# A hybrid mixer with its norms, keys, values and attention laid out anew, in a residual block on one core

## What is computed

```python
proj = einsum('btd,dc->btc', rmsnorm(x), w_in)        # 2048 -> 7184 columns
# attention, blocks of 128 queries, q, k, v raw:
z = q @ k.T * scale; valid = s_idx < t_idx
log_1m = where(valid, log_sigmoid(-z), 0)
later = cumsum(log_1m, reverse=True) - log_1m
att = where(valid, exp(log_sigmoid(z) + later), 0)
o_sb = rmsnorm(att @ v, sb_out_gain)
# delta rule: q, k, v through a width-4 convolution and silu; q and k L2-normed
g = cumsum over the chunk of the log gates; decay = exp(g_i - g_j)
L = where(strict, (k * beta) @ k.T * decay, 0)
T_mat = inverse(I + L); u = T_mat @ (v * beta); w = T_mat @ (k * beta * exp(g))
# per chunk: v_new = u - w @ S; o = (q * exp(g)) @ S + qk @ v_new; S updated
o_dn = rmsnorm(o, dn_out_gain) * silu(dn_z)
h = x + rmsnorm(concat(o_sb, o_dn) @ w_out)
```

## Time and profile before

| | us |
|---|---|
| median of 3 runs | 1363.92 (1348.13 to 1617.84) |
| the profiled execution | 1355.06 |
| its span | 1353.3 |
| PE busy | 1294.6 (96%) |
| DVE busy | 940.7 (70%) |
| ACT busy | 708.2 (52%) |
| POOL busy | 228.8 (17%) |
| moved by DMA | 225.85 MB, mean 167 GB/s |

### The profile page before, as it was taken

One profiled execution on the slowest core, in us unless ns is written; L12 is line 12 of the kernel. 1 busy time (PEld: TensorE's weight loads), 2 busy tenths in 40 slices (PEclk: granted clock), 3 DMA queues, 4 the chain that ended last, 5 costly groups with the idle time before them and its releaser, 6 DMA issues.

```text
span 1353.3 us, 20838 instructions
## 1 busy us (share of the span) xinstructions
PE 1294.6 (96%) x6906; PEld 1088.4 (80%) x6906; DVE 940.7 (70%) x1703; ACT 708.2 (52%) x1288; POOL 228.8 (17%) x293
## 2 busy tenths in 40 slices
PE   5999979999999979989999999999999999999996
PEld 4676769857888757878888888888888888888885
DVE  5697696646765535566978888888788885555554
ACT  5454444424434664546566656665666555444442
POOL 5321120122201130000222322232222220000000
PEclk9899989979999988999999999999999999999999
DMA  8352543313633403553555455554555556555551
GB/s 329 124 204 108 139 175 119 131 63 123 199 116 127 167 19 125 191 183 124 191 201 197 178 194 187 186 190 182 206 176 202 179 199 221 197 202 188 187 186 62
DMA packets 32695, 225.85 MB, mean 167 GB/s; under 512 B 4352, under 2 KB 4736, under 8 KB 5888
## 3 DMA queue, kind: packets, MB, share of 16 engines
q1 hardware_dynamic: 30528, 218.12, 45.2%
q10 hardware_dynamic: 2112, 7.00, 2.1%
HBM read 222.87 MB, written 2.23 MB: 166 GB/s over the span
## 4 chain that ended last, share of the span: by engine, by line
PE 87%; DVE 8%; ACT 2%; issue 1%; DMA 1%; ACTq 1%; POOL 0%; DVEq 0%; SPq 0%; POOLq 0%
PE bank L1219 35%; PE bank L1221 17%; PE bank L1508 8%; PE bank L1510 8%; PE bank L1509 8%; DVE w_lo L752 3%; ACT w_hi L409 1%; DVE arena L777 1%; PE bank L1302 1%; PE bank L1255 1%; PE bank L1373 1%; PE bank L1313 1%; PE bank L1273 1%; DVE ssum L822 1%; DMA raw<-in_wts 1%
## 5 line engine op out<-in xcount | busy, mean ns | idle before, releaser
L1219 PE MATMUL bank<-xhl,w_hi 128*128 128x512 f32 x2304 | 826.6, 403 | 21.3 <-DVE w_lo L752 15.9
L752 DVE TENSOR_TENSOR w_lo<-raw,w_hi 128x512 fp32r<-128x512 f32 x816 | 574.9, 727 | 250.2 <-ACT w_hi L409 248.0
L409 ACT ACTIVATE w_hi<-raw 128x512 fp32r<-128x512 f32 x816 | 500.4, 628 | 392.2 <-PE bank L1221 233.8
L1221 PE MATMUL bank<-xhl,w_lo 128*128 128x256 f32 x2304 | 645.7, 280 | 0.0
L1219 PEld LDWEIGHTS bank<-xhl,w_hi 128*128 128x128 f32 x2304 | 437.3, 190 | 140.3 <-issue 20.8
L1221 PEld LDWEIGHTS bank<-xhl,w_lo 128*128 128x128 f32 x2304 | 438.8, 190 | 0.1
L1508 PE MATMUL bank<-w_hi,ffn_act 128*128 128x512 f32 x352 | 136.9, 389 | 0.0
L1510 PE MATMUL bank<-w_hi,ffn_act 128*128 128x512 f32 x352 | 136.9, 389 | 0.0
L1509 PE MATMUL bank<-w_lo,ffn_act 128*128 128x512 f32 x352 | 136.9, 389 | 0.0
L381 POOL TENSOR_TENSOR arena<-arena,token_scale 128x256 f32<-128x256 f32 x88 | 79.4, 918 | 308.8 <-DVE arena L757 186.4
L1141 DVE SCALAR_TENSOR_TENSOR arena<-arena,fcw 128x256 f32<-128x256 f32 x176 | 85.3, 485 | 23.9 <-DVE arena L1141 1.5
(11 more groups left out here) (230 smaller groups left out, 847.1 us busy)
## 6 DMA issues: line engine op xcount, KB each, us to landing
raw<-in_wts SPq DMA_DIRECT2D x204, 1024.0 KB, 4.7
xfeat<-in_x SPq DMA_DIRECT2D x4, 512.0 KB, 9.5
xfeat<-in_x_tok ACTq DMA_DIRECT2D x1, 2048.0 KB, 7.8
arena<-base_rows ACTq DMA_DIRECT2D x16, 128.0 KB, 5.0
out_y<-xfeat SPq DMA_DIRECT2D x4, 512.0 KB, 2.9
arena<-in_post_gains ACTq DMA_DIRECT2D x1, 1024.0 KB, 4.7
down_gain<-in_post_gains ACTq DMA_DIRECT2D x1, 1024.0 KB, 4.7
arena<-in_w_ba ACTq DMA_DIRECT2D x1, 320.0 KB
```

The source lines that it names most:

```text
L409: nc.scalar.activation(w_hi[:, i % RING, :], raw[:, slot, quarter * PIECE:(quarter + 1) * PIECE], ACT.Copy).then_inc(hi_ready, 1)
L752: V.tensor_tensor(w_lo[:, i % RING, :], raw[:, slot, quarter * PIECE:(quarter + 1) * PIECE], w_hi[:, i % RING, :].bitcast(f32), ALU.subtra ...
L1219: M(ps[j][:, :], w_hi[:, r % RING, w], xhl[:, k, :, :].rearrange("p a t -> p (a t)"), start=(k == 0), stop=False, skip_group_check=True)
L1221: last = M(ps[j][:, 0:T], w_lo[:, r % RING, w], xhl[:, k, 0, :], start=False, stop=(k == KT - 1), skip_group_check=True)
```

## The change

It rewrites the mixer; nothing that is computed changes, but nearly every step's layout and place does.

- **Token groups.** `FEAT_GROUPS = 10`: the first ten input groups (dn q, k, v of batch 0, the same of batch 1, sb q and k) stay feature pieces. The last four (sb v, two groups; dn z, two groups) become token pieces, in banks (0,1) and (2,3) in turn. ACT alone empties these, two 512-wide operations a group that also apply the token's norm, and silu for z (`token_evac`, L471).
- **Input.** ACT rounds x times its gain in one operation, DVE forms the rest in one; POOL has no part in it. The sum of squares of x comes from a token-major copy of x (ACT, 2 x 2048 elements with accumulation), and one 256-column matmul at slot 18 spreads it.
- **Gates.** 64 matmuls of 32 or 16 columns at slot 14 give logits with tokens on partitions; beta, gates, their sums and the norms are then columns `col[128 x 16]`. Gate differences come back through DRAM as a broadcast load.
- **Norms.** Keys are not normed: the factors go into the triangular system (`CNEG`), with squares from transposed keys (ACT, accumulating, L1361 for the transposes). Sums with 8 columns and spreads with 8 rows (L1293, L1302, L1313, L1263, L1420, L1465, L1524) are gone.
- **Batches** start at slots 44 and 112. The block loads are 2 instead of 8 a batch. Spreading the base blocks (L374) and level masks (L332) are on POOL, 512 wide. The first tap of each convolution is on ACT.
- **Attention** runs in two rounds of four heads from slots 181 and 200, between token pieces. Its output is token-major, normed there, transposed back (16 transposes); the same for z times o (`z_turn`, one batch at slot 214, one inside the first output group). The output projection reads a tile of its own, `mix_hl`.

```diff
-            def conv_tile(g, j):
...
-                    else:
-                        ins = V.tensor_scalar(conv[:, j, :], proj[:, t, :], w, None, ALU.mult)
-                    ins.then_inc(s("conv_done") if lag == 3 else s("conv_step"), 1)
+            def conv_tile(c, j):
...
+                dve.wait_ge(s("conv_first"), n_ + 1)
+                for lag in range(1, 4):
...
+            def token_evac(g):
...
+                    dst, func = (vtok, ACT.Copy) if n_ < 2 else (ztok, ACT.Silu)
+                    nc.scalar.activation(dst[:, j, 512 * (n_ % 2):512 * (n_ % 2) + 512], ps[token_banks(g)[j]][:, :], func,
+                                         scale=stat[:, 3, j:j + 1]).then_inc(s("tok_evac"), 1)
...
+            follow(PLACE["ba"])
+            pe.wait_ge(s("wba_lo"), 1)
...
+                for k in range(KT):
+                    M(ps[5][:, 64 * j:64 * j + 32], xhl[:, k, 0, js], wba_hl[:, k, :, :].rearrange("p a n -> p (a n)"),
+                      start=(k == 0), stop=False, skip_group_check=True)
+                    last = M(ps[5][:, 64 * j:64 * j + 16], xhl[:, k, 1, js], wba_hl[:, k, 0, :],
+                             start=False, stop=(k == KT - 1), skip_group_check=True)
...
+                for g in range(2):
+                    follow(PLACE["kt", b, g])
...
+                    turn(lambda r: chunk(1, 4 * g + r), ps[4 + g], "kt_mm")
+                    follow(PLACE["kk", b, g])
...
+                        last = M(ps[6 + g][:, r * P:(r + 1) * P], k_, k_, start=True, stop=True)
...
-            follow(SB_PLACE)
-            pe.wait_ge(s("sbq"), HEADS)
...
-            for h in range(EARLY):
-                sb_z(h)
-            follow(16 * IN_GROUPS)
+            for r in range(BATCHES):
+                heads = range(BH * r, BH * r + BH)
+                for h in heads:
+                    sb_z(h)
+                pe.wait_ge(s("tri_ready"), 2)
+                for h in heads:
+                    sb_c(h)
+                for h in heads:
+                    sb_av(h)
...
-            for i in range(HEADS // 2):
-                pe.wait_ge(s("son_rstd"), 1)
-                for a in range(2):
-                    last = M(ps[4 + i][:, a * T:(a + 1) * T], sel[:, 2 * i + a, :], nrow, start=True, stop=True)
-                last.then_inc(s("son_bc"), 1)
```

More of the change, by code:

```diff
@@ L50, in down_bank @@
     return (4 + 2 * c + j) % 8
[L53 to L56, removed]
-    for _i in range(BASE):
[L58 to L69, removed]
-    for _i in range(2 * LEVELS):
[L71 to L74, removed]
+PLACE = {"ba": 14, "stat": 18, "gcum": 24, "grow": 26, "gload": 28}
@@ L493, in step @@
                 act_e.wait_ge(s("act_step"), n[0])
+            follow(PLACE["stat"] + 2)
             act_e.wait_ge(s("ba_sb"), 1)
-            nc.scalar.activation(small[:, 0, :], small[:, 0, :], ACT.Exp, scale=-1.0).then_inc(s("eb"), 1)
-            step(nc.scalar.activation(small[:, 1, :], small[:, 1, :], ACT.Identity, bias=gate[:, 1:2]))
-            step(nc.scalar.activation(small[:, 2, :], small[:, 1, :], ACT.Abs))
-            step(nc.scalar.activation(small[:, 3, :], small[:, 2, :], ACT.Exp, scale=-1.0))
@@ L530, in _ @@
+                for g in range(2):
+                    follow(PLACE["turn", b, g] + 1)
                     act_e.wait_ge(s("turned"), 2 * b + g + 1)
@@ L559, in sb_exp @@
+                for u in range(UNITS):
+                    ins = nc.scalar.activation(squares[:, u, :], otok[b][:, u, :], ACT.Square, accum_out=c_(OO, 8 * b + u))
+                ins.then_inc(s("o_sq"), 1)
+                follow(PLACE["rs", b] + 1)
+                act_e.wait_ge(s("o_inv"), b + 1)
+                nc.scalar.activation(col[:, RS, block_n(b)], col[:, RS, block_n(b)], ACT.Sqrt).then_inc(s("o_root"), 1)
             def sb_exp(h):
@@ L1272, in _ @@
-            for k in range(KT):
-                last = M(ps[5][0:40, 0:T], wba[:, k, :], full[:, k, :], start=(k == 0), stop=(k == KT - 1))
-            last.then_inc(s("ba_done"), 1)
-            follow(40)
-            pe.wait_ge(s("bg_row"), 1)
-            pe.wait_ge(s("ke_row"), 1)
-            for n_, (r, j) in enumerate(((1, 0), (1, 1), (0, 0), (0, 1), (2, 1), (3, 0))):
-                last = nc.tensor.transpose(ps[6][:, 8 * n_:8 * n_ + 8], rows[:, r, j * P:(j + 1) * P], ident[0:8, 0:8])
@@ new lines, in sb_ot, with z_turn @@
+            def sb_ot(h):
+                follow(PLACE["ot", h])
+                pe.wait_ge(s("so_tok"), h + 1)
+                for j in range(NJ):
+                    js = slice(j * P, (j + 1) * P)
+                    last = nc.tensor.transpose(ZB[h % BH][:, T + j * P:T + (j + 1) * P], SO_TOK[h % BH][:, js], ident[:, :])
+                last.then_inc(s("ot_mm"), 1)
+            def z_turn(b, g):
+                pe.wait_ge(s("z_mix"), 2 * b + g + 1)
+                turn(lambda r: otok[b][:, 4 * g + r, :], ps[2 * b + g], "zturn_mm")
```

1496 lines of the change are left out of this document (771 added, 725 removed).

## The result

The changed kernel takes 1294.55 us (median of 4, 1293.84 to 1295.3), the kernel before 1356.03 (median of 4). The ratio is 0.956, with a 95% interval of 0.951 to 0.961: 4.4% faster, where the forecast was 1271 and thus 6.2%. The time lies in the range, 24 us above the likeliest value. One of the four executions of before took 1617.84 us and is left out of the ratio (the other three took 1342.57, 1348.13 and 1363.92); why it was so slow is not known.

What follows compares the result with a forecast made beforehand. PE was taken to bound the kernel. Work to attention's end 405.6 (from 10 us) + waits 21 + clock 5 = 431.6, + output projection 88 + unchanged rest 750.3 + 1.8 = 1271.7 us; range 1244 to 1308.

Steps and rivals of the forecast that it cites:

- parts 1, 2, 4: PE's work up to attention's end: input pieces 225.6 + 87.0 us, batch steps 54.8 for 89, attention 20.2 replacing 35.60.
- Part 3: Statistics and gate logits: 64 narrow matmuls at 0.11 us each, 7.1; 8.0 with sums of x and gates.
- Part 5: PE's waits from 10 us to the end of attention: 21 us together; lower bound 2, upper today's 35 plus 5.
- x by tokens: Wait at the start for loading the 2 MB token-major copy of x: 0 to 5 us, taken as 2.5.
- the block rows: Waits for DVE's row operations and POOL's spread and masks in the batches: 3 us for batch 0, 1 for batch 1.
- the rounds: Waits in the two attention rounds: 2 x 2.6 us for the sums' inputs and 3 for norms, 8 together.
- Part 6: Lower granted clock to attention's end: only the start's two windows stay, 2.25 + 2.75 = 5 us lost; the others go.
- the last rival: Lower clock stays for a third of the stage through short steps and transposes; 1390 us at 30%; above 1330, chance 0.04.
- part 7: Output projection takes 88 us for 94.4; from 603 us, and the 1.8 us around the span, nothing moves.
- waits stay as large as now: Rounds and block rows cost today's 35 us for 21, clock 15 for 5: 1296 us; 1285 to 1305, chance 0.23.
- The case in which the chain rules the rounds: Pieces between attention steps hide nothing; 12 to 17 us return in each round: 1305 to 1330 us, chance 0.07.
- The slower rival: Same as the last rival: gain gone with 21% of the stage's PE work at lower clock, over 2% slower from 28%.

Runs made afterwards that it cites:

- e3: Changed kernel with the store of packed blocks and their load issued by SP in place of ACT; 1292.16 us, ratio 0.9507 to the kernel before.
- e12: Changed kernel with block DMA on SP, logits in four lots, region at 91584, v transposes two slots and attention's cumulative sums one slot later; 1271.41 us, ratio 0.9357.
- e1: The kernel before, unedited, profiled again on the chip of the next three kernels; span 1352.8 us.
- e2: The changed kernel, unedited, run again on the same chip as the rerun of the kernel before; 1297.30 us, ratio 0.9554.
- e5: Changed kernel with the region of xhl, ffn_act, mix_hl and arena moved 128 bytes later, to 91584; median 1288.45 us, ratio 0.9495.
- e6: The kernel before with the region of the big operands moved 128 bytes later, to 91712; 1369.47 us, one execution.
- e7: Changed kernel with block store and load issued by SP and the gate logits in four lots; 1285.37 us, ratio 0.9486.

## Why the prediction came out as it did

- **The direction and PE's list** (parts 1, 2, 4) held. 395.6 us of work and 5 of clock were forecast for the stage; PE was busy 410.5, of which the lower clock is 9.1 (5 forecast) and the token pitch 2.1 (384 x 0.0055); 3.7 are left over, 1% of the list, and no run says of which part. Emptying on ACT cost PE nothing (but 0.9 us in front of the first product with v), spread on POOL 1.8 us.
- **Part 3** held in price: the narrow matmuls start every 0.11 us at full clock, the first half of them; the second half fell into the low clock and took 0.21 each, so that the block took 10.2 us (31.5 to 41.7) for the 7.1 forecast.
- **Part 5, waits**: 21 forecast, 20.5 measured, but the sum is right by luck. x by tokens cost 0 of its 2.5, the block rows 1.8 of 4, the rounds 5.4 of 8. The 8.4 us in front of v and the 2.4 in front of the sums of the gates were not seen: I priced the row stretch on DVE and not the packing just ahead of it, and did not name what is queued behind ACT's wait for it. e3 showed that half of the 8.4 is the store, its flight and the load on ACT, and e12 that with these on SP two slots more take the longest wait from 4.0 to 1.4.
- **Part 6, clock**: 5 forecast, 9.1 measured. The start cost 5.0 as taken; the 2.3 at 126 to 131 us stand behind the gap of 8.4, the 1.8 at 407 to 411 behind one of 1.9. Part 5 had priced new gaps, and part 6 put no low clock behind any of them. The 34 us that it and the last rival take for today's low clock are too few: the 0.90 and 0.95 of attention and output projection are 2 x (3.6 + 4.7) = 17 more.
- **"From 603 us ... nothing moves"** (part 7) is the step that was wrong. The loops moved by 12 us and the output projection by 2.3 (90.3 for 88), through 128 bytes of address (e1, e2, e5, e6). In sum: 9.4 us at the end of attention (4.1 clock, 2.1 pitch, -0.5 waits, 3.7 rest), 2.3 in the output projection, 11.9 behind it, less 1.5 because I cut the kernel before at 603 instead of 604.5: 22.1, from 1271.7 to 1293.84.
- **Rivals.** The time of 1294.55 is nearly that of "waits stay as large as now" (1296), but not by its mechanism: waits were 20.5, not 35. The case in which the chain rules the rounds has a time that its sum does not give: 2 x 12 to 17 us above 1271.7 is 1296 to 1306, and 1320 to 1330 only on top of the larger waits; the rounds cost 5.4 us of waits. The slower rival did not occur: with 88 transposes placed at the batches and rounds the clock was 1.00 from 60 to 120 and from 150 to 390 us in the first profile, and in e2's the two stretches of 3.5 us at 62 and 93 us come to 7 us and not to a third of the stage. The Trainium skill, "TensorE: Matmul & The Clock Gate", section "Part 4: PE-mode transpose", says that a transpose does not count as busy time for the clock in the same way. At this density the traces show no cost of it; no run took the transposes out.
- **The table load.** The Trainium skill, "ScalarE: Activation LUTs", section "What ACT_TABLE_LOAD costs", adds a drain of about 1.38 us to each switch. The trace does not agree: in the first round of attention the activation again starts 0.02 us behind the load, with no drain:

```profile
360.94 1.28 ACT L672 ACT_TABLE_LOAD   x1
362.24 1.76 ACT L672 ACTIVATE arena<-arena 128x384 f32<-128x384 f32 x4
```

## What to carry to other kernels

When a change shortens or lengthens any tensor ahead of the big operands, the matmuls' pitch can change by 1 to 2.5% with nothing else touched: compare the start-to-start time of matmuls in a loop that was not edited before explaining a difference, and pin the address. That settled the token matmuls here, but not the pairs, which had two pitches at the best address. A step that is moved between pieces must be asked for late enough, one or two slots here, since a gap can be followed by half speed: the one of 8.4 us and the last of 1.9 us were in both profiles of the changed kernel, those of 2.4 and 1.6 to 1.9 us at 60 and 91 us in one of the two. An engine that issues a DMA from computed data holds up all that stands behind it in its list, by the wait for the data and the flight (8.4 us of PE's time here, 4.0 with the DMA on SP): give it to a queue that has slack.

## What the runs showed of the hardware that I had not expected

- The pitch of 512-column fp32r matmuls at full clock takes three values, 0.2267, 0.2288 and 0.2324 us, with the start of the region of xhl and ffn_act in the partition (rests of 192, 128 and 64 bytes in 256; two addresses each for the first and the last, one for the middle). Why is open. In token pieces it is the stationary operand that lies in the region and in feature pieces the moving one, while the weights did not move; but the arena with what DVE, ACT and POOL read and write moved along, and no run parts that from PE's own operands.
- With a rest of 192 the pairs of feature pieces run at 0.347 or 0.353 us, and change between the two within an execution; what throws them over is open. No run tried the rest of 0.
- A stretch at 1.2 GHz comes between 28 and 51 us in the profiles of both kernels: some 3 us long in e1_before, 7 in e7 and e12, 14 in e3 and 10 in the others, with a gap ahead (before) or with none (after, where PE was busy all 25 us from 10 to 35). What brings it is open.
